# Turning x on VectorE in an encoder layer: loads, turns, stores and scaling at other places in the order

## The reference

```
h = rmsnorm(x, g_pre_mix) * (1 + scale1) + shift1
proj = h @ w_in                      # q,k,v,o of 4 mLSTM heads, gates, q,k,v of 8 attention heads
hm = mlstm_chunkwise(...) forward + backward, normalised, gated
hn = neighbourhood_attention(...)    # on a 16 x 64 grid
x = x + gate1 * rmsnorm(concat(hm, hn) @ w_out, g_post_mix)
```

## Time and profile before

| | |
|---|---|
| median of 3 runs | 2347.81 us (2345.64 to 2349.93) |
| the profiled execution | 2346.43 us, its span 2344.6 us |
| PE busy | 2238.1 us, 95% |
| DVE busy | 1410.6 us, 60% |
| the stretch of the change | about 263 to 410 us of the span |

### The profile page before, as it was taken

How to read it: one execution, slowest core, us unless ns; L and a number is a source line. 1 busy time by engine, 2 the same in 40 slices (tenths; PEclk the granted TensorE clock), 3 DMA queues, 4 the chain that set the end, 5 groups by cost and what they waited for, 6 DMA issues and landing times. The chain is left out here.

```text
span 2344.6 us, 34389 instructions
## 1 busy us (share of the span) xinstructions
PE 2238.1 (95%) x13051; PEld 1861.2 (79%) x13051; DVE 1410.6 (60%) x2069; ACT 1097.2 (47%) x1768; POOL 750.6 (32%) x770
## 2 busy tenths in 40 slices
PE   6999999999999999999993999999999999999997
PEld 4679978977899888677772888888888888888886
DVE  3213354555413436665558777777778778888885
ACT  4213442555433435666542445444444445555553
POOL 3003332433233415341003422112222335443534
PEclk9999999999999999999996999999999999999998
DMA  8837785757554449764637576666666679999996
GB/s 317 268 112 231 220 231 170 220 147 190 140 186 153 153 157 245 213 202 142 203 130 273 215 248 229 225 218 225 226 225 228 225 260 310 312 320 322 320 302 230
DMA packets 234878, 524.06 MB, mean 224 GB/s; under 512 B 38964, under 2 KB 138180, under 8 KB 215280
## 3 DMA queue, kind: packets, MB, share of 16 engines
q1 hardware_dynamic: 185360, 407.37, 51.5%
q0 software_dynamic: 49376, 114.78, 17.7%
HBM read 423.71 MB, written 97.88 MB: 222 GB/s over the span
## 5 line engine op out<-in xcount | busy, mean ns | idle before, releaser
L2667 DVE TENSOR_TENSOR moe_w_lo<-moe_wf,moe_w_hi 128x2048 fp32r<-128x2048 f32 x192 | 436.7, 2287 | 196.1 <-ACT moe_w_hi L2523 195.1
L2523 ACT ACTIVATE moe_w_hi<-moe_wf 128x2048 fp32r<-128x2048 f32 x192 | 365.8, 1915 | 376.4 <-PE moe_acc L2853 362.2
L2853 PE MATMUL moe_acc<-moe_w_hi,moe_x_hi 128*128 128x512 f32 x1024 | 398.8, 389 | 0.9 <-DVE moe_x_lo L2673 0.6
L2853 PE MATMUL moe_acc<-moe_w_lo,moe_x_hi 128*128 128x512 f32 x1024 | 398.4, 389 | 0.0
L2853 PE MATMUL moe_acc<-moe_w_hi,moe_x_lo 128*128 128x512 f32 x1024 | 398.4, 389 | 0.0
L2853 PEld LDWEIGHTS moe_acc<-moe_w_hi,moe_x_hi 128*128 128x128 f32 x1024 | 192.2, 188 | 41.4 <-DVE moe_x_lo L2673 0.8
L2853 PEld LDWEIGHTS moe_acc<-moe_w_hi,moe_x_lo 128*128 128x128 f32 x1024 | 192.2, 188 | 40.1
L2853 PEld LDWEIGHTS moe_acc<-moe_w_lo,moe_x_hi 128*128 128x128 f32 x1024 | 192.2, 188 | 39.7
L2397 POOL DMA_INDIRECT moe_xe<-scratch_h,moe_parts x120 | 195.3, 1627 | 87.4 <-issue 76.2
L1874 PE MATMUL banks<-fr_w_hi,fr_h_hi 128*128 128x256 f32 x768 | 222.9, 290 | 0.0
L1874 PE MATMUL banks<-fr_w_lo,fr_h_hi 128*128 128x256 f32 x768 | 217.0, 283 | 0.0
(11 more groups left out here) (322 smaller groups left out, 4374.3 us busy)
## 6 DMA issues: line engine op xcount, KB each, us to landing
moe_wf<-in_w_expert_gate SPq DMA_DIRECT2D x64, 1024.0 KB, 5.7
moe_wf<-in_w_expert_up SPq DMA_DIRECT2D x64, 1024.0 KB, 5.1
moe_wf<-in_w_expert_down SPq DMA_DIRECT2D x64, 1024.0 KB, 6.9
fr_w_raw<-in_w_units SPq DMA_DIRECT2D x28, 1024.0 KB, 6.6
fr_bias<-in_na_bias SPq DMA_DIRECT2D x16, 1520.0 KB, 11.6
fr_a_w<-in_w_ada POOLq DMA_DIRECT2D x16, 1024.0 KB, 8.3
scratch_qk_t<-fr_stage SPq DMA_DIRECT2D x64, 256.0 KB, 2.7
scratch_vov<-fr_stage SPq DMA_DIRECT2D x96, 128.0 KB, 2.3
```

The lines of the kernel that those rows point to most:

```text
L2523: nc.scalar.activation(w_hi[:, q, :, :], wf[:, q, :, :], ACT.Copy).then_inc(w_hi_ready, 1)
L2667: nc.vector.tensor_tensor(w_lo[:, q, :, :], wf[:, q, :, :], w_hi[:, q, :, :].bitcast(F32), ALU.subtract).then_inc(w_lo_ready, 1)
L2853: mm = nc.tensor.matmul(acc[:, j, b, :], x[:, g, k, :], w[:, q, a, h * HALF:(h + 1) * HALF], start=(k == 0 and i == 0), stop=(k == KC - 1 ...
```

## The change

The four loads of x move from blocks 32, 35, 38, 41 to 33, 36, 39, 42. At blocks 33 and 39 a head begins, and in SP's program its loads come ahead of the block's own. The turning moves three ticks later, to the second and third tick of blocks 34, 37, 40, 43. The stores move to blocks 36, 39, 42, 45, each just ahead of the next step's load. `load_xt(2)` moves from block 46 to 48, the spreading of the norms for the last 512 tokens from tick 208 to 216, and `scale_x(2, k)` from ticks 196 to 203 to ticks 204 to 211. `load_xt(3)` and `scale_x(3, k)` stay.

```
-XQ_AT, XQ_STEP, XQ_STEPS = M1 - 25, 3, 4
-XT_AT = {2: M1 - 11, 3: M1}
-SPREAD_AT = {2: (M1 - 11) * TICKS, 3: (M1 - 5) * TICKS}
-SCALE_AT = {2: (M1 - 8) * TICKS, 3: (M1 + 2) * TICKS}
+XQ_AT, XQ_STEP, XQ_STEPS = M1 - 24, 3, 4
+XT_AT = {2: M1 - 9, 3: M1}
+SPREAD_AT = {2: (M1 - 11) * TICKS, 3: (M1 - 3) * TICKS}
+SCALE_AT = {2: (M1 - 6) * TICKS, 3: (M1 + 2) * TICKS}
...
                             step, late = divmod(b - XQ_AT, XQ_STEP)
+                            if late == 0 and 0 < step <= XQ_STEPS:
+                                store_xq(step - 1)
                             if late == 0 and 0 <= step < XQ_STEPS:
                                 load_xq(step)
-                            if late == 2 and 0 <= step < XQ_STEPS:
-                                store_xq(step)
...
                         step, late = divmod(b - XQ_AT - 1, XQ_STEP)
-                        if late == 0 and 0 <= step < XQ_STEPS and u >= 2:
-                            turn_xq(step, u - 2)
+                        if late == 0 and 0 <= step < XQ_STEPS and u in (1, 2):
+                            turn_xq(step, u - 1)
```

## The result

The changed kernel takes 2367.63 us (median of 4 runs, 2366.81 to 2372.24) against 2348.77 us for the one before (4 runs, 2345.64 to 2349.93): ratio 1.0086, interval 1.0069 to 1.0104, so 18.9 us slower. The profiled executions have spans of 2365.2 and 2344.6 us, 20.6 us apart. 5.9 us slower was forecast, and 2363 was the upper end of the range.

A forecast was written before the change was run, and what follows sets the result against it. TensorE, busy 95% of the span, was taken as the bound. New waits and clock of 15.1 us less 9.2 removed gave 5.9 us slower: 2352.3 us, 2353.7 on the median's scale, range 2343 to 2363.

The forecast's parts named there:

- The two waits of line 2072: TensorE's waits for a head's k and q behind x, heads 1 and 2: 1.73 and 0.90 us, counted as gone.
- the two of line 2082: TensorE's waits for VectorE's `scores` in heads 1 and 2: 1.39 and 3.78 us, counted as gone.
- Its price, up to 4.7 us: Eight scalings among `finish_head(3)`'s last pieces, costed at nothing; at most 4.7 us without cover; rival's chance 0.02.
- how long the step's four loads need from the first issue to the turn: Time for x, taken from whole steps before: 8.43 us, and 9.38 for the first step.
- slow landing: Rival: behind the head's loads and stores every step needs 11.72 us; 12 to 20 us more; chance 0.10.
- first step, line 2103: TensorE's step of chunk 3 waits for its state, queued behind VectorE's turn: 1.1 us new wait.
- second step, line 2091: Head 1, `turn_o` of chunk 6: TensorE waits for line 1705 behind VectorE's turns: 3.98 us new wait.
- third step, line 1865: Block 41 in head 2: TensorE waits for `split_w`, directly behind VectorE's turn: 2.53 us new wait.
- fourth step, line 2091: Same as the second step but in head 2, wanted in `turn_o`: 3.98 us new wait.
- clock, for all four: TensorE's lower clock after new waits: 1.39 us for each wait of 3.98, 0.7 for the 2.53, none for 1.1.
- the 9.2 removed: Four old TensorE waits in heads 1 and 2, 7.80 us, plus 1.39 us of clock: 9.19 us gone.
- The port rule: 32 partitions reach 8 of 16 ports, some 218 GB/s: 6.8 us for 1 MB of x, 3.5 us faster.

The follow-up runs named there:

- the tail alone: Kernel before, with only `load_xt(2)`, the spreading and the scaling moved to where the change has them: 2348.62 us, ratio 1.0.
- the first run: Changed kernel with loads of x a block earlier, ahead of the head's loads, stores moving with them, turns as changed: 2352.22 us, ratio 1.0012.
- the stores apart: Changed kernel with stores of x two blocks behind their load instead of just ahead of the next load: 2360.37 us, ratio 1.0051.

## Why the prediction was wrong in size

**Right: the mechanism and its places.** The two waits of line 2072 and the two of line 2082 went. As forecast, line 2091 waits in chunk 6 of heads 1 and 2 for line 1705, the projection waits once for `split_w`, and the step of chunk 3 waits for its state: four places named, four found, with their releasers. All are VectorE's wait for x. The scaling waits 1.41 us for its x at 420.59 with no wait of TensorE's behind it, and the tail alone costs nothing that can be measured. (Its price, up to 4.7 us, was set too low: line 1437 takes 0.74 us eight times in the trace before, 5.9 us.) One forecast sign failed: line 1430 was to wait 7 to 10 us for x each time, and waited 17.18, 6.32, 15.23 and 8.61.

One reading was too simple. I said that VectorE's waits for x became TensorE's 1.39 and 3.78. In the run with the tail alone VectorE has x in time in the second step, and TensorE still waits 0.89 us there. So most of the 1.39 was not the wait for x, presumably it was the turns themselves, queued ahead of `scores`. The sum does not depend on this.

**The step that failed** is "how long the step's four loads need from the first issue to the turn": 8.43 us, and 9.38 for the first. Measured were 14.71, 8.96, 11.12 and 9.16. I took the least of the whole steps before, on the ground that nothing big is now issued right behind x. What counts is which loads lie ahead. Ahead of the first step are now the head's loads and 1 MB of weights, ahead of the third the head's loads; the run with x ahead of the weights gave 2.5 us back at once, and with x ahead of the head's loads too, in the first run, both steps were under 9.8. The store just ahead costs its 3 us of issue, which the prediction had. The rival "slow landing" had the right row (11.72 us, with a weights' load ahead) and 0.10 of the chance. It was true of the first and third step only; that its 12 to 20 us more take in the measured 18.9 is partly luck.

| wait | forecast | measured |
|---|---|---|
| first step, line 2103 | 1.1 | 4.83 |
| second step, line 2091 | 3.98 | 4.31 |
| third step, line 1865 | 2.53 | 6.37 |
| fourth step, line 2091 | 3.98 | 5.27 |
| clock, for all four | 3.5 | about 7.1 |
| sum | 15.1 | 27.9 |

The clock's 7.1 is the 5.7 us above plus the 1.39 that the one old wait had cost. Less the 9.2 removed the sum is 18.7, as the stretch shows. So the waits were forecast 9.2 us too short, 7.6 of it in the first and third step, and the clock 3.6.

The landings were 5.33, 0.53, 2.69 and 0.73 us longer than reckoned, 9.28 in sum, which is the 9.2. That it comes out so evenly is luck, since other terms were off and cancel. In the first step x was issued 12.05 us ahead of the moment at which TensorE wanted the state (272.03 against 288.91 - 4.83), not 10.2 as reckoned. Without x ahead of them the head's loads and the store behind them took SP 7.48 us up to the weights' load (263.50 to 270.98) instead of 10.26 (265.93 to 276.19). This hid 1.9 us of the longer landing. In the third step x was issued 7.15 us ahead of that moment (334.69 against 348.21 - 6.37) instead of 8.33, which added 1.2.

**The clock** was forecast too low, for two reasons. Two waits that I held too short to cost any or much became 4.83 and 6.37 us long. And a wait can cost more than the 1.39 us of the single example. It can be read from the matmuls: after the wait of 4.31 those of line 1865 follow each other by 0.43 us until 319.3, and by 0.23 after; after the wait of 6.37 the slow pace lasts until 353.4, 5.2 us. At half the clock that is some 1.9 and 2.6 us lost. After 4.83 it is some 1.5 (to about 292.0) and after 5.27 some 1.4 (to about 381.0), 7.4 in all, close to the 7.1 left over above. Nor was half the price right for a wait of some 2.5 us. In the first experiment's trace the slow pace after a wait of 2.81 us lasts 3.8 us, so it cost some 1.9:

```profile
365.38 0.66 PE L2091 MATMUL banks<-fr_ident,fr_og 128*128 128x128 f32 x4 [2.81 <-DVE fr_E L1705]
369.21 0.47 PE L1865 MATMUL banks<-fr_h_hi,fr_w_lo 128*128 128x512 f32 x1
369.52 0.40 PE L1865 MATMUL banks<-fr_h_hi,fr_w_hi 128*128 128x512 f32 x1
```

The 9.2 us counted as removed fit what was measured: with the turn a block later 10.3 us are won between the medians and 8.4 between the spans.

The port rule of the Trainium skill (SBUF — State Buffer, "Door 1: the DMA port swizzle") gave 6.8 us for the loads and a faster kernel. (The 2 us in it stand in that page's next section, "The DMA setup-cost knee".) As a rate it agrees with the trace: 206 GB/s in the window from 280 to 284 us of the changed kernel, where mostly x is moved, near the 218 of the page. As a time for the step it doesn't: 14.71 us with the loads ahead, which aren't in it, and no step that VectorE waited for was under 7.92 us in any run (the fourth with the other order of the loads).

The 20.6 us between the two spans are not all the change's. At 1100 us (last matmul of line 2046) the changed kernel is 17.7 us later than the one before, and the kernel with the turn a block later is 9.9 us earlier. From there to the end these two take 1247.1 and 1245.7 us, the kernel before 1244.2, and the one with only the tail moved 1245.6. So some 2.9 of the 20.6 us between the two spans arise there, and about half of that is also in the traces of the other two; what makes it was not looked for.

What stays open: how the loads ahead delay x. The bytes moved grow with the landing in the first step, but a store ahead adds as many and costs little, so bytes alone don't tell it. No run parts the bytes from the order in the queue or from the kind of transfer.

## What to carry to other kernels

Place an instruction that waits for a transfer by what is queued behind it on its engine, and count the transfer's time with the loads ahead of it in its queue, not from the issue or from a quiet example. To move a load behind urgent ones can pay, but what waits for it must then move by the whole new landing time. Here half of the move cost 18.9 us, and a block more turned it into a gain of 10.3. The four new waits of TensorE, 4.3 to 6.4 us long, were paid about one and a third times (27.9 us for 20.8), and one of 2.8 us in another run cost some 1.9 us more than its length.

## What had not been expected of the hardware

The issue itself is slower the more is ahead. Four loads of 256 KB took SP 2.19 us with little ahead of them, 3.13 and 2.71 us behind a head's loads and the block's small stores (the runs with x ahead of the weights and with the stores apart), 3.61 and 3.47 us behind a store alone, and 5.86 and 5.50 us behind a head's loads and another 1 MB, be it the weights or a store. Everything behind them in SP's program moves with it. But the slow issue is not what makes the landing long: in the third step it fell from 5.50 to 2.71 us, and x was turned 11.55 instead of 11.12 us after its first issue. And the price of TensorE's clock did not go by the length of the wait: about 1.9 us after 2.81 and after 4.31 us of waiting, and about 1.4 us after 5.27, where the slow pace ended within 2.9 us (at 381.0 after 378.09).
